# A two-block mixer model on one core: fewer columns in the input projection, six norms' squares summed on VectorE, and another order at the end of attention

## The reference, cut to what matters

```python
def first_block(x, p, ...):
    z = rms_norm(h, pre_mix_norm) @ w_in            # 2834 columns: RWKV 1408, NSA, S5 256
    mix = concat([rwkv7(token_shift(z_rw)), nsa(z_nsa), s5(z_s5)]) @ w_out
    h = h + rms_norm(mix, post_mix_norm)            # norm 1 in the kernel
    f = conv_ffn(rms_norm(h, pre_ffn_norm))         # norm 2; hidden width 2816
    h = h + rms_norm(f, post_ffn_norm)              # norm 3
    e = rms_norm(p @ w_ple, ple_norm)               # norm 4
    return h + sigmoid(h @ w_ple_gate) * e

def second_block(x, c, ...):
    # layer 0: pooling mixer, layer 1: dilated attention over three branches, 16 heads of 64
    h = modulate(rms_norm(x), shift, scale)         # norms 5 and 7 (7 also for the keys and values)
    x = x + g1 * mixer(h)
    x = x + g2 * conv_ffn(modulate(rms_norm(x)))    # norms 6 and 8
    return rms_norm(x)                              # norm 9
```

## Time and profile before

| | us |
|---|---|
| median of 3 runs (1453.73 to 1458.12) | 1455.54 |
| the profiled execution | 1459.26 |
| its span, first to last instruction | 1457.3 |
| TensorE matmuls busy | 1362.4 |
| ScalarE busy | 619.2 |
| VectorE busy | 562.4 |
| GpSimd busy | 833.8 |

### The profile page before, as it was taken

How to read it: one execution, slowest core, us unless ns; L and a number is a source line. 1 busy time by engine, 2 the same in 40 slices (tenths; PEclk the granted TensorE clock), 3 DMA queues, 4 the chain that set the end, 5 groups by cost and what they waited for, 6 DMA issues and landing times.

```text
span 1457.3 us, 26522 instructions
## 1 busy us (share of the span) xinstructions
PE 1362.4 (93%) x11138; PEld 1277.3 (88%) x11138; DVE 562.4 (39%) x1241; ACT 619.2 (42%) x925; POOL 833.8 (57%) x419
## 2 busy tenths in 40 slices
PE   6989798979899999989999999999999987999998
PEld 5987355868899999989999999989999877999997
DVE  4645867651255472322433302132233242333301
ACT  3532153223465554544444434544544343554431
POOL 5872430022388878545688775845655443688771
PEclk9998798996899999989999999999999999899998
DMA  7945898330455555434455554443636683455550
GB/s 219 207 123 188 301 383 312 120 112 4 134 171 185 175 180 179 140 108 149 141 177 193 166 188 146 140 132 91 186 91 216 192 286 102 158 178 192 167 159 30
DMA packets 246323, 244.96 MB, mean 168 GB/s; under 512 B 25652, under 2 KB 215230, under 8 KB 246206
## 3 DMA queue, kind: packets, MB, share of 16 engines
q1 hardware_dynamic: 245715, 243.10, 52.2%
q10 hardware_dynamic: 491, 0.17, 0.1%
HBM read 242.20 MB, written 1.05 MB: 167 GB/s over the span
## 4 chain that ended last, share of the span: by engine, by line
PE 83%; DVE 6%; issue 2%; ACT 2%; DMA 2%; POOL 0%; DVEq 0%; ACTq 0%
PE banks L533 82%; DVE arena L1584 2%; DMA ring<-in_attn_w_o_dram 1%; DVE arena L1591 1%; ACT arena L2291 1%; DMA ring<-in_ffn_w_up_dram 1%; PE banks L543 0%; DVE banks L1591 0%; ACT ring_hi L2291 0%; DVE ring_lo L1584 0%; DVE arena L1772 0%; PE banks L818 0%; DVE arena L1588 0%; DVE hn L1591 0%; PE banks L941 0%
## 5 line engine op out<-in xcount | busy, mean ns | idle before, releaser
L1535 POOL TENSOR_TENSOR ring_lo<-ring,ring_hi 128x2048 fp32r<-128x2048 f32 (+1 forms) x176 | 718.7, 4096 | 510.4 <-ACT ring_hi L2291 510.0
L533 PE MATMUL banks<-hn_hi,ring_lo 128*128 128x256 f32 x1888 | 539.1, 289 | 0.0
L533 PE MATMUL banks<-hn_hi,ring_hi 128*128 128x256 f32 x1696 | 484.4, 290 | 7.6 <-ACT hn_hi L2291 7.6
L533 PE MATMUL banks<-hn_lo,ring_hi 128*128 128x256 f32 x1696 | 445.0, 283 | 0.0
L2291 ACT ACTIVATE ring_hi<-ring 128x2048 fp32r<-128x2048 f32 (+1 forms) x176 | 299.7, 1704 | 179.7 <-PE banks L533 131.0
L533 PEld LDWEIGHTS banks<-hn_hi,ring_lo 128*128 128x128 f32 x1888 | 375.2, 199 | 0.0
L533 PEld LDWEIGHTS banks<-hn_hi,ring_hi 128*128 128x128 f32 x1696 | 335.0, 198 | 9.6 <-issue 9.4
L533 PEld LDWEIGHTS banks<-hn_lo,ring_hi 128*128 128x128 f32 x1696 | 310.9, 193 | 0.1
L2291 ACT ACTIVATE arena<-banks 128x256 f32<-128x256 f32 (+5 forms) x229 | 90.3, 411 | 319.1 <-PE banks L533 265.4
L533 PEld LDWEIGHTS banks<-arena 64*128 64x128 f32 (+4 forms) x1282 | 122.7, 188 | 72.4 <-issue 52.3
L533 PE MATMUL banks<-arena 128*64 128x128 f32 (+9 forms) x1282 | 150.4, 314 | 32.1 <-issue 13.2
(11 more groups left out here) (236 smaller groups left out, 1706.0 us busy)
## 6 DMA issues: line engine op xcount, KB each, us to landing
ring<-in_ada_w_dram SPq DMA_DIRECT2D x48, 1024.0 KB, 8.3
ring<-in_ffn_w_up_dram SPq DMA_DIRECT2D x44, 1024.0 KB, 5.2
ring<-in_w_up_dram SPq DMA_DIRECT2D x22, 1024.0 KB, 5.1
ring<-in_ffn_w_down_dram SPq DMA_DIRECT2D x16, 1024.0 KB, 5.4
ring<-in_w_kv_dram SPq DMA_DIRECT2D x15, 1024.0 KB, 5.4
ring<-in_w_kv_dram SPq DMA_DIRECT2D x18, 512.0 KB, 3.9
ring<-in_attn_w_q_dram SPq DMA_DIRECT2D x18, 512.0 KB, 3.9
ring<-in_w_in_dram SPq DMA_DIRECT2D x8, 1024.0 KB, 12.1
```

The costliest lines, as they stand in the source:

```text
L533: return nc.tensor.matmul(o, l, r, start=start, stop=stop, **k)
L1535: led.emit(g.tensor_tensor(low, raw, high.bitcast(F32), ALU.subtract), sem("lo_ready"))
```

## The change

- Input projection: keys are two chunks whose columns stand once (kc and vc, ks and kw); a tile holds both groups, and ScalarE copies each half to where it is needed (four activations per tile). The gates are one channel-major tile of 18 rows, transposed after tanh. The first norm's squares and sums are ScalarE's, from the token-major x; x tile 3 is copied by ScalarE. Chunk 0 is loaded right after x, its lower half is GpSimd's; p and all later rows are SP's, behind chunk 1. Lower halves on VectorE are ordered anew.
- Norms 1, 3, 6, 7, 8, 9: ScalarE writes square 0 into a held PSUM bank and the others singly; VectorE adds squares 1 to 5 to it, the last sum going to square 0's place in SBUF; TensorE multiplies only 0, 6 and 7, all behind the last tile.
- Attention: the diagonals move to ScalarE, the first two tile shares to both sides of turn 0, ada steps to rounds 7 to 12, and `out_begun(2)` to rounds 13, 14 and 15. In the late rounds ScalarE does upper halves only where `reach` is written out.

```diff
-        for i, (c0, c1) in enumerate(((KC_COL, KC_COL + HD), (VC_COL, VC_COL + HD), (KS_COL, KS_COL + HD),
-                                      (KW_COL, KW_COL + HD))):
-            chunk_src["keys", i] = [kmaj(w_in, c, c + HD) for c in (c0, c0, c1, c1)]
-        early = [("in", i) for i in range(8)] + [("keys", i) for i in range(4)] + [("gate", 0), ("u", 0)]
+        chunk_src["keys", 0] = [kmaj(w_in, KC_COL, KS_COL)]
+        chunk_src["keys", 1] = [kmaj(w_in, KS_COL, VS_COL), kmaj(w_in, KW_COL, VW_COL)]
+        early = [("in", i) for i in range(8)] + [("keys", 0), ("keys", 1), ("gate", 0), ("u", 0)]
...
+        SUMMED = (1, 3, 6, 7, 8, 9)
+        square_base, square_count = {}, 0
+        for i in NORM_ORDER:
+            square_base[i] = square_count
+            square_count += 8 if i in SUMMED else 0 if i == 4 or i == 0 else 5
...
-        SHARES = (3, 4, 4, 5, 4, 4, 4, 5, 4, 4, 4, 5, 4, 0, 0, 0)
+        FIRST_SHARE, SHARES = 2, (2, 4, 4, 5, 4, 4, 4, 5, 4, 4, 4, 5, 3, 0, 0, 0)
...
+            def gathered(i):
+                numbered(("acc", i), held_back())
...
+                    if key == early[0]:
+                        pe.wait_ge(sem("first_lo"), 1)
+                    elif key in early:
+                        pe.wait_ge(sem("early_lo"), early.index(key))
...
             def mean_square_of(i, b, sq, ks):
                 for k in ks:
-                    if k % 2 == 0 or k == KT - 1:
-                        pe.wait_ge(sem("squares"), 5 * (i - (i > 4)) + (1, 1, 2, 2, 3, 3, 4, 5)[k])
+                    if i in SUMMED and k == 0:
+                        copied(("acc", i))
+                    elif i in SUMMED:
+                        pe.wait_ge(sem("squares"), square_base[i] + k + 1)
+                    elif k % 2 == 0 or k == KT - 1:
+                        pe.wait_ge(sem("squares"), square_base[i] + (1, 1, 2, 2, 3, 3, 4, 5)[k])
                     for s in range(2):
                         last = mm(b[:, s:s + 1], sq[:, k, s * P:s * P + P], ones_mean[:, 0:1],
                                   start=(k == s == 0), stop=(k == KT - 1), skip_group_check=True)
                 if ks[-1] == KT - 1:
                     close(last)
+                    if i in SUMMED:
+                        held.remove(bank_no["acc", i])
...
-                mean_square_of(ms[0], b_ms, ms[1], (0, 1, 2, 3, 4, 5))
                 w = chunk(key)
                 for k in range(KT):
                     last = three_passes(b[:, 0:T], [v[:, k, 128:256] for v in w], [v[:, k, :] for v in x],
                                         k == 0, k == KT - 1)
                 close(last)
-                mean_square_of(ms[0], b_ms, ms[1], (6, 7))
+                mean_square_of(ms[0], b_ms, ms[1], (0, 6, 7))
...
-            pe.wait_ge(sem("mean_ready"), 1)
-            mean_square(0, hn)
...
-                for i in range(4):
-                    split_tile((nm, i), ("keys", 2 * x + i // 2), 128 * (i % 2), xz)
-            split_rows(("gtok",), [(slice(s * 18, s * 18 + 18), slice(s * P, s * P + P)) for s in range(2)],
-                       ("gate", 0), xz)
+                for i in range(2):
+                    split_tile((nm, i), ("keys", x), 128 * i, xz)
+            split_tile(("gT",), ("gate", 0), 0, xz, 18)
             for i in range(2):
                 split_tile(("u", i), ("u", 0), 128 * i, xz)
+            copied(("gT",))
+            turn(("gtok",), [gate_rows[:, s * P:s * P + P] for s in range(2)])
...
+            for _ in range(FIRST_SHARE):
                 next(coming, None)
             for i in range(16):
                 if i < 15:
...
                 if i > 0:
                     dil_values(i - 1)
                 dil_turn(i)
-                for _ in range(SHARES[i] if i else 0):
+                for _ in range(SHARES[i]):
                     next(coming, None)
-                if 8 < i < 14:
+                if 6 < i < 13:
                     ada()
                 if i == 13:
-                    for n in range(2):
-                        in_turn(("do", n))
-                    ada()
-                if i == 14:
                     ada_columns(True)
-                if i >= 14:
+                if i >= 13:
                     out_begun(2)
             dil_values(15)
-            out_begun(2)
...
+            gathered(8)
             for m, bank in enumerate(out_banks):
                 numbered(("dw", m), bank)
                 held.remove(bank)
-                close(out_passes(m, bank, (6, 7)))
+                close(out_passes(m, bank, (6, 7)), 1 if m else 2)
...
+                if n == 1:
+                    sp.wait_ge(sem("stage_clear"), 2)
+                    stage_rows(sp, soon[0::2], sem("soon_in"))
+                if n == 2:
+                    sp.dma_start(ptok, a["p"][0, 0].rearrange("(s p) d -> p s d", p=P)).then_inc(sem("ple_in"), 16)
+                    stage_rows(sp, later, sem("later_in"))
+                    sp.dma_start(dt_rows[0:8, :],
+                                 a["s5_log_dt"].rearrange("l (j g) -> (l j) g", g=2)).then_inc(sem("later_in"), 16)
...
+            raw, low, high = chunk_flat(early[0])
+            pool.wait_ge(sem("early_hi"), 1)
+            led.emit(g.tensor_tensor(low, raw, high.bitcast(F32), ALU.subtract), sem("first_lo"))
...
+            def add_square(i, k, sq):
+                acc = bank_of(("acc", i))[:, 0:T]
+                dve.wait_ge(sem("squares"), square_base[i] + k + 1)
+                if k == 1:
+                    take(("acc", i))
+                else:
+                    own_done(summed_at[i, k - 1])
+                if k < 5:
+                    tt(acc, sq[:, k, :], acc, ADD)
+                    summed_at[i, k] = led.count["dve_own"]
+                else:
+                    tt(sq[:, 0, :], sq[:, k, :], acc, ADD, *freed(("acc", i)))
...
+            early_low(2)
...
-                if i % 2 == 0:
-                    early_low(i // 2 + 2)
                 b = take(("rw", i))
                 dve.wait_ge(sem("shift_own"), i + 1)
                 stt(zs[:, i, 1:T], b[:, 0:T - 1], col("mu", i), zs[:, i, 1:T], MUL, ADD, *freed(("rw", i)))
+                if i % 2 == 1:
+                    early_low(i // 2 + 3)
+            early_low(8)
...
+                        if 2 <= m <= 6:
+                            add_square(7 if f == 1 else 9, m - 1, hn)
...
-                rec(dst[:, i % 4, 2, :], dst[:, i % 4, 1, :])
-                settle()
-                for x in range(2):
-                    ts(inv_sum[:, s, x, :], ident[:, :], dst[:, i % 4, 2, x:x + 1], MUL, signal=sem("dil_inv"))
+                rec(dst[:, i % 4, 2, :], dst[:, i % 4, 1, :], sem("dil_rec"))
...
+            def summed_squares(i, dst_, after):
+                sqrt_table()
+                for k in range(KT):
+                    after(k)
+                    o = dst_[:, k, :] if k else take0(("acc", i))[:, 0:T]
+                    af(o, h[:, k, :], ACT.Square, sem("squares"))
...
-            squares(hn, lambda k: act_.wait_ge(*freed(("xT", k // 2))))
+            act_.wait_ge(setup_in, 16)
+            for s in range(2):
+                af(hn[:, 4 * s:4 * s + 4, :].rearrange("p a b -> p (a b)"), xtok[:, s, :], ACT.Square, scale=1.0 / 32,
+                   accum_out=rs[:, s:s + 1])
+            settle()
+            af(rs[:, 0:2], rs[:, 0:2], ACT.Sqrt, sem("first_root"), bias=eps_col)
+            b = take0(("xT", 3))
+            af(h[:, 6:8, :], shaped(b, 2, T), ACT.Identity, *freed(("xT", 3)))
...
+            high_parts(0, 0, hn_hi)
             early_high(1)
-            root(0)
-            high_parts(0, 0, hn_hi)
+            act_.wait_ge(sem("derived"), 1)
+            early_high(2)
...
+                for g in range(2):
+                    group = b[64 * g:64 * g + 64, :]
+                    af(kcs[0:64, 2 * i + g, :], group[:, 0:T])
+                    af(kcs[64:128, 2 * i + g, 0:T - 1], group[:, 1:T], ACT.Identity,
+                       *(freed(("kc", i)) if g else (None, None)))
             def kd_(i):
                 b = take(("kd", i))
-                af(kd[:, i, :], b[:, 0:T], ACT.Identity, *freed(("kd", i)))
+                for g in range(2):
+                    for x in range(2):
+                        af(kd[64 * x:64 * x + 64, 2 * i + g, :], b[64 * g:64 * g + 64, 0:T], ACT.Identity,
+                           *(freed(("kd", i)) if g == x == 1 else (None, None)))
...
+            def gate_(_):
+                b = take(("gT",))
+                af(gate_rows, b[0:18, 0:T], ACT.Tanh, *freed(("gT",)), scale=0.5)
...
-                if 1 <= c < len(early) - 1:
+                if 2 <= c < len(early) - 1:
...
-            squares(hn, lambda k: gone(("po", k)))
+            summed_squares(6, hn, lambda k: gone(("po", k), 99 if k < 6 else 0))
...
+            def dil_inverse(i):
+                s = i % 2
+                if i >= 2:
+                    act_.wait_ge(psum_ready, job_no["dp", i - 2, 1, s] + 1)
```

(16 more changed lines are left out.)

100 lines of the change are left out of this document (50 added, 50 removed).

## The result

The changed kernel takes 1443.8 us (median of 7 runs, 1436.4 to 1447.2); beside it on the same chip the kernel before took 1453.7 (1450.1 to 1458.1). The ratio is 0.9925, 95% interval 0.9897 to 0.9952: faster by 0.75%, some 10 us. The forecast was 1396, with 1380 to 1416 as its range. The time lies far outside it: five sixths of the forecast gain are missing. One execution of one later run (set 2, the gates between the keys) took 2102 us at a mean granted clock of 0.55 and is left out of that run's figures.

The account below looks back on a forecast made before the run. TensorE, busy 93% of the span, was taken as the bound. Gains of 25 + 13.7 + 4.7 + 18 = 61.4 us gave 1397.9 from the profiled 1459.3, 1394 from the median 1455.5; forecast 1396, range 1380 to 1416.

Parts of the forecast that it names:

- part 2: Six norms: squares 1 to 5 summed on VectorE, 20 TensorE instructions fewer each; 13.7 us for norms 1, 3, 6, 7, 9.
- rival 4: Attention rounds: ScalarE waits for VectorE's reciprocal and writes diagonals, delaying copies and upper halves; 1475 at 5 us a round; chance 0.03.
- The last sentence of the forecast: Wrong if ScalarE's new order delays upper halves in rounds full today, or the front's GpSimd chain is slower than its rows.
- part 4: Attention's end, 1177.2 to 1249.8 us: waits, norm 8's mean-square instructions and half clock shrink; gain 18 us, bounds 8 and 23.
- a wait of 3.1: Attention's end: TensorE still waits 3.1 us for the last query copy, plus 1.7 of clock.
- Rival 2: Attention's end keeps its waits in new places, ScalarE waiting in order for out chunks; gain 7, total 1407; chance 0.13.
- Part 1: Input projection: removed work, clock, fewer holes and earlier start; gain 25 us, bounds 18 and 31.
- the two new holes: Input projection: TensorE waits for upper and lower halves, 3.2 us ahead of keys 1 and 3.1 us ahead of u.
- The sums themselves: Norms' mean squares added on VectorE: 2.74 us each, 13.7 for five norms; norm 8's 2.7 counted at attention's end.
- Part 3: Attention's begin: two tiles moved behind turn 0 cover the second turn's wait; gain 4.7 us, bounds 0 and 4.7.
- rival 1: Input projection paced by the halves, or sines after 46 us; 12 us less gain there, total 1408; chance 0.20.
- rival 3: The new holes don't appear or don't lower the clock; 8 us better, total 1388; chance 0.15.

Follow-up runs that it names:

- set 2: Four runs on first run of set 1's kernel: lower parts to GpSimd 1400.9 us; no upper halves ahead in round 12, 1408.3; both 1402.5; gates between keys 1405.0.
- first run of set 1: Changed kernel with the upper halves ahead of down tiles 6 and 7 brought back at norms 3 and 7, sums kept: 1409.5 us, ratio 0.9683.
- first run of set 2: Kernel of the first run of set 1 with attention's six lower parts moved from VectorE to GpSimd: 1400.9 us, ratio 0.9646.
- first run of set 3: Kernel of first run of set 1 with lower parts on GpSimd and no upper halves ahead of round 12's probability and query copies: 1401.8 us, ratio 0.9648.

## Why the prediction was wrong

**The step that failed: part 2, what ScalarE pays in the norms.** The forecast read the change of the squares as "about 0.2 us for each pair of squares split, with the same slack" and counted the instructions. It did not ask what the added `take0` and the limit of 0 for tiles 6 and 7 take away: they are the places at which ScalarE writes the next projection's first upper halves. So the term was put at nothing, without a reason. What is moved there is work: three upper halves at each norm, which now stand in a row of four, behind norm 3 and in the middle of norm 7's upper parts, and GpSimd's lower halves behind them. The description of the kernel has the rule: `reach(job)` converts all chunks whose buffers are free by then; and the trace of the kernel before has these three halves between the last down tiles, in idle time of ScalarE. The price was 37 us in the kernel before (36.8) and about 35 in the changed one, more than half of the forecast gain. No rival had it: rival 4 looked for late ScalarE rounds in attention. The last sentence of the forecast names late upper halves as a sign of being wrong, but for full rounds, and gives them neither a place in the norms nor a price.

**The second: part 4, the size of attention's end.** The forecast had 18 us; the trace shows 4.5, and the exchange of the old end for the new one is worth 0 of 15.3. The term was mis-sized in its residue: "a wait of 3.1" for the last query's copy. It is 4.3 in the changed kernel, and its cause is named in part only: the copy does stand behind upper halves of out chunks, but these had landed. What was late is the first out chunk, for which ScalarE stood 8.4 us ahead of round 12's copy. Where that stand was taken out (set 2), the halves did wait for their chunks as the forecast has it, and the wait was 4.33. Not foreseen at all is the wait of 6.38: the lower parts on VectorE, moved by a round to where GpSimd does the out chunks' halves, took 12.5 us in place of the 2.1 that the same six took in the kernel before, with round 14's scores behind them. The forecast cited the rule on the shared port for the diagonals alone and did not put it to the six instructions that the change moved. Rival 2 (waits in new places, part 4 at 7) comes near it, at 7 us where it was 4.5, but names ScalarE and the out chunks only, which is the smaller of the two waits.

**What was right.** Part 1: 25 against 25.2; the first matmul was forecast at 18.3 and came at 17.02, the two new holes at 3.2 and 3.1 against 2.87 and 4.68, the end of u at 99 against 99.9. The last hole is longer because the lower half took 3.66 us on VectorE in place of 2.3; it began at 87.59, while a GpSimd instruction ran until 89.10. That part 1 is right to 0.2 us is partly luck: the start came 1.3 us sooner than forecast and the last hole was 1.6 us longer. The sums themselves: 6 x 2.74 = 16.4 against 15.2, with 0.24 us of wait for norm 7's last square in place of 0.68; but they are not alike, norm 1's gave 4 us or more. Part 3: 4.7 against 4.8. The forecast's rival 1 (the projection paced by halves) did not come about, and rival 3 (no new holes) neither.

With the measured terms the forecast's sum would have been 25.2 + 12.7 + 4.8 + 4.5 - 36 = 11.2 us, where 12.7 is five sixths of the 15.2 and 36 lies between the two prices of the limit; the runs say 10. Of the 51 us that are missing, the first step has some 36 and the second 13.5.

**What is shown and what is argued.** The holes at norms 3 and 7 are shown by taking the edit out and by putting it in alone. That the last wait at attention's end, 6.15 us, hung on the first out chunk's upper half is shown by the run that moves this half alone. The wait of 5.41 us behind VectorE's lower parts had a cause of its own, and did not come back once they were moved. That the diagonals brought nothing is shown for the kernel with GpSimd's lower parts, not for the changed kernel itself. What the gates' place brings is shown in the traces, for the hole and for the projection's end (some 5 us); in the whole time it is 3 and 7 us by two pairs of ratios (0.9683 to 0.9660, 0.9648 to 0.9602), and the intervals of both pairs overlap. Why norm 1's sum is worth more than the others is not shown.

## What to carry to other kernels

Where a helper does work "on the way" (upper halves inside `take`), a limit or a variant without it is a move of that work: find where it goes next and what stands behind it there, in idle time of the engine as well as in busy time. Where a wait is removed and one as long stands elsewhere, suspect one chain; look for its first late member and for a gap in which its input has already arrived, before more covers are piled on it. And before VectorE's subtractions of two SBUF tiles, or its diagonals, are moved, see what GpSimd does at the new place. When medians can't tell a small edit, compare the stretch of the trace that it touches.

## What the runs showed of the hardware

VectorE beside a running GpSimd subtraction of 128x2048 (4.5 to 4.7 us), first run of set 1: of six subtractions of 128x256 with both inputs in SBUF the three that met one took 2.12, 4.76 and 4.71 us and ended some 0.3 us behind it; the three that came after took 0.41 each. In the first run of set 2 one instruction of 8 columns with both inputs in SBUF took 4.65 us. What kept its time beside GpSimd in that trace: instructions with one operand in PSUM (0.20 us for 24 columns, six of 128 columns in 1.28 us), a reciprocal of 2 columns (0.17), and a maximum over 1536 columns with its one input in SBUF (1.75 us, as long as without GpSimd). The six subtractions on GpSimd took 4.16 us in all, and no wait of TensorE ended with them in that run; in the first run of set 3 one did (6.15 us).

Behind the idle 20.6 us the granted clock stood at 0.50 for the following 5.1 us, in which one tile of 24 matmuls took the whole time; and after 17.6 us at 0.71 over 5.4 us.
